# Feed-forward up projections of a decoder trunk as seven Strassen block products, on one Trainium2 core

## The reference

```python
D_MODEL = 1024; SEQ = 512; DEPTH = 2; DEC_BATCH = 8; N_A = 1
D_FF = 2816
def swiglu_ffn(x, w_in, w_out):
    gate, up = jnp.split(x @ w_in, 2, axis=-1)      # w_in 1024 x 5632
    return (jax.nn.silu(gate) * up) @ w_out         # w_out 2816 x 1024
def run(x, ...):
    for l in range(DEPTH):
        if l == N_A:
            kv = rms_norm(x, kv_norm) @ w_kv        # k (with rope) and v
        x = x + 0.5 * swiglu_ffn(rms_norm(x, norm_ffn[l, 0]), ffn_w_in[l, 0], ffn_w_out[l, 0])
        h = rms_norm(x, norm_mix[l])
        mix = conv_module(h, ...) if l < N_A else diff_attention(rope(h @ w_q), k, v) @ w_o
        x = x + mix
        x = x + 0.5 * swiglu_ffn(rms_norm(x, norm_ffn[l, 1]), ffn_w_in[l, 1], ffn_w_out[l, 1])
    return rms_norm(x, norm_final), ...
```

## Time and profile before

| | us |
|---|---|
| median of 3 runs | 2078.97 (2078.32 to 2080.6) |
| span of the profiled execution | 2076.1 |
| PE busy | 2031.0 (98%) |
| DVE busy | 916.6 (44%) |
| ACT busy | 677.6 (33%) |
| POOL busy | 500.2 (24%) |

### The profile page before, as it was taken

One profiled execution on the slowest core, in us unless ns is written; L12 is line 12 of the kernel. 1 busy time (PEld: TensorE's weight loads), 2 busy tenths in 40 slices (PEclk: granted clock), 3 DMA queues, 4 the chain that ended last, 5 costly groups with the idle time before them and its releaser, 6 DMA issues.

```text
span 2076.1 us, 39794 instructions
## 1 busy us (share of the span) xinstructions
PE 2031.0 (98%) x16292; PEld 1959.6 (94%) x16292; DVE 916.6 (44%) x1087; ACT 677.6 (33%) x1083; POOL 500.2 (24%) x343
## 2 busy tenths in 40 slices
PE   8999999999799999999999999999988999999998
PEld 7999999988599999999999999999965799999997
DVE  5444333499853333333543333333578543333323
ACT  4222222455542222222233222222256432222211
POOL 1333310133123333210312333300321223333210
PEclk9999999999999999999999999999999999999999
DMA  6333333288333333332553333322676133333331
GB/s 198 92 91 91 102 98 94 75 163 169 75 92 92 91 91 91 108 98 68 155 144 101 91 91 91 114 86 84 184 233 225 41 92 91 91 91 97 100 98 42
DMA packets 358735, 224.19 MB, mean 108 GB/s; under 512 B 8035, under 2 KB 342244, under 8 KB 358508
## 3 DMA queue, kind: packets, MB, share of 16 engines
q1 hardware_dynamic: 340836, 193.89, 31.5%
q0 software_dynamic: 8496, 18.93, 4.7%
q10 hardware_dynamic: 9320, 10.20, 1.7%
HBM read 198.52 MB, written 7.53 MB: 99 GB/s over the span
## 4 chain that ended last, share of the span: by engine, by line
PE 87%; DVE 7%; issue 2%; DMA 2%; ACT 1%; POOL 0%; DVEq 0%; ACTq 0%; SPq 0%; POOLq 0%
PE ps_all L567 84%; DVE conv_b L1390 1%; DVE conv L1390 1%; DVE kprod L1586 1%; DVE s_dec L1592 1%; PE ps_all L742 1%; PE ps_all L692 1%; DMA made<-made 1%; PE ps_all L660 1%; DVE w_lo L1208 1%; DVE nmx L1522 0%; DMA made<-sq 0%; DMA x<-xT 0%; DVE x L1336 0%; PE ps_all L624 0%
## 5 line engine op out<-in xcount | busy, mean ns | idle before, releaser
L873 ACT ACTIVATE w_hi<-raw 128x1024 fp32r<-128x1024 f32 (+1 forms) x295 | 333.5, 1130 | 1223.3 <-PE ps_all L567 1208.2
L567 PE MATMUL ps_all<-xg_hi,w_hi 128*128 128x260 f32 x3456 | 700.4, 284 | 10.0 <-DVE xg_lo L1218 9.0
L567 PE MATMUL ps_all<-xg_hi,w_lo 128*128 128x260 f32 x3456 | 697.3, 283 | 0.0
L567 PE MATMUL ps_all<-xg_lo,w_hi 128*128 128x260 f32 x3456 | 696.3, 283 | 0.0
L567 PEld LDWEIGHTS ps_all<-xg_hi,w_hi 128*128 128x128 f32 x3456 | 534.6, 189 | 12.2 <-issue 10.1
L567 PEld LDWEIGHTS ps_all<-xg_hi,w_lo 128*128 128x128 f32 x3456 | 533.7, 189 | 0.0
L567 PEld LDWEIGHTS ps_all<-xg_lo,w_hi 128*128 128x128 f32 x3456 | 532.5, 189 | 0.0
L1208 DVE TENSOR_TENSOR w_lo<-raw,w_hi 128x1024 fp32r<-128x1024 f32 (+1 forms) x295 | 397.1, 1346 | 259.1 <-ACT w_hi L873 259.1
L567 PE MATMUL ps_all<-h_hi,w_hi 128*128 128x260 f32 x1664 | 343.7, 284 | 7.0 <-DVE h_lo L1457 6.7
L567 PE MATMUL ps_all<-h_hi,w_lo 128*128 128x260 f32 x1664 | 341.3, 283 | 0.0
L567 PE MATMUL ps_all<-h_lo,w_hi 128*128 128x260 f32 x1664 | 340.7, 282 | 0.0
(11 more groups left out here) (204 smaller groups left out, 1106.7 us busy)
## 6 DMA issues: line engine op xcount, KB each, us to landing
raw<-w_in SPq DMA_DIRECT2D x175, 512.0 KB, 3.7
raw<-w_out SPq DMA_DIRECT2D x64, 704.0 KB, 4.2
made<-made POOLq DMA_DIRECT2D x41, 256.0 KB, 5.7
raw<-c_in SPq DMA_DIRECT2D x16, 512.0 KB, 3.8
raw<-w_kv SPq DMA_DIRECT2D x16, 512.0 KB, 3.9
page<-cache_k SPq DMA_DIRECT2D x16, 512.0 KB, 4.4
page<-cache_v SPq DMA_DIRECT2D x11, 512.0 KB, 5.5
t_out<-t_gate ACTq DMA_DIRECT2D x64, 65.0 KB, 2.7
```

The lines of the kernel that those rows point to most:

```text
L567: mm = nc.tensor.matmul(unit[slot][:, s, :], w[:, c % 2, k * P:(k + 1) * P], m[:, s * HALF:(s + 1) * HALF], start=kk == 0 and i == 0, stop ...
L873: nc.scalar.activation(w_hi[:, c % 2, 0:w], raw[:, c, 0:w], ACT.Copy).then_inc(hi_made, 1)
```

## The change

The up projections are computed by the Strassen-Winograd scheme. The product of `w_in` (split into rows (input features) and columns (gate, up)) and of x (split into feature halves and token halves) is a 2x2 block product. It is made of seven block products, whose operands are sums of blocks, and seven additions of results. The 1/rms factor of the gate is applied at the output, as before; that of the up side is no longer multiplied in by POOL but applied to the result of down, in which the hidden tiles are linear.

**Groups and items.** A group makes two gate and two up tiles. It has seven items (`product`), one per block product, each of 4 feature pairs x 3 products x 2 output tiles = 24 matmuls of 260 columns: 168 per group, where the same outputs took 192. Each item takes one w_hi, w_lo buffer of a ring of three. A feed-forward part has 11 groups, in three parts of 8, 8 and 6 hidden tiles (4, 4 and 3 groups), each followed by its own down phase of 8 chunks with 8, 8 or 6 tiles: up, down, up, down, up, down. Each down phase adds into x.

**Token sums.** For each of four pairs of x tiles, ACT copies both tiles into `stage` (`copy_x`), DVE makes four sums there (N1, T3, N2, T4; `combine_x`, 128x260 each), ACT rounds all seven operands (`combos_hi`, 1820 elements per partition) and DVE makes the rests (`combos_lo`). There is one `stage`: the next pair begins when the rests are done. The last pair goes in five segments.

**Weight sums.** Five loads of 512 KB per group (block W21 twice), then four accumulating DMAs of 512 KB by POOL: S3 = W21 + W11 and S1 = W21 + W22 when the loads are in, S2 = W11 + S1 when item 0 is split, S4 = W12 + S2 when item 1 is split and S2 is done. There are 10 slots, two sets of five; slots 0 to 3 of the first set are also the ring of the plain chunks. A slot is filled again once the last item that reads it has been split (`FREED_BY`). The groups of a feed-forward part take the second set and the first in turn, the second first (in the first part of the third feed-forward part the first set first), so that the last group of a part of 4 has the first set, and that of a part of 3 the second; there it is the other way round. After item n ACT and DVE split item n+2 (`step`), which needs the ring's buffer of item n-1.

**Results.** DVE takes PSUM in seven additions per group (`add`, 128x2x260), then gate times rstd, the product with `up_sum` and the rest h_lo, each for two tiles at once; ACT copies the first product, makes SiLU and rounds. POOL does no arithmetic in these phases. In down, DVE takes each chunk times rstd and adds it in a second instruction. All hardware loops are written out.

```diff
+PARTS = (8, 8, 6)
+PART_AT = (0, 8, 16)
+RING = 3
+PAIRS = KD // 2
...
+N1, N2, T3, T4, B21, B22, B11, B12 = range(8)
+STEPS_OF = (B11, B21, T3, N2, N1, T4, B22)
+SEGMENTS = ((B11, B12), (B21, B11), (T3, T4), (N1, T3), (T4, B21))
+SEGMENT_OF = (0, 1, 2, 3, 3, 4, 1)
+TAKEN_BY = (None, 1, 3, 2, 5, 6, 7)
+IN_A_SET = PAIRS - 1 + len(SEGMENTS)
...
+        W11, S1, W22, S3, W12 = range(5)
+        BLOCK_OF = (W11, W12, S3, W11, S1, W22, W12)
+        FREED_BY = {S3: 2, S1: 4, W22: 5, W11: 6, W12: 6}
...
+                for blk in (W11, S3, S1, W22, W12) if first_in else (S3, S1, W22, W11, W12):
+                    s = blk + 5 * in_second(ph, g)
...
+                    need[s] = ph.chunk0 + ITEMS * g + FREED_BY[blk] + 1
+            for c in range(ph.chunks):
+                s = c % 4
+                filled[s] += 16
+                landed[ph.chunk0 + c] = (s, filled[s])
+                of_phase.append((s, need[s], ph.weights(c)))
+                need[s] = ph.chunk0 + c + 1
...
+        def bank_of(g, i):
+            return (0, 2, 4, 6, 2, 0, 4)[i] if g % 2 == 0 else (6, 2, 4, 0, 2, 6, 4)[i]
...
+            def product(ph, g, i, q, pairs=range(PAIRS)):
+                n, room = ph.chunk0 + ITEMS * g + i, rooms[ph.f]
+                bank, ring = bank_of(g, i) + q, n % RING
+                if pairs[0] == 0 and q == 0:
+                    pe.wait_ge(weights_ready, n + 1)
+                    if i < 2 and not g:
+                        if ph.unit0:
+                            pe.wait_ge(drained, ph.unit0 - 1 + i)
+                    elif i < 4 and g:
+                        pe.wait_ge(taken, sums_of(ph, g - 1, (5, 4, 6, 5)[i]) if i else sums_of(ph, g - 1, 3))
+                    elif i == 5:
+                        pe.wait_ge(p1_copied, ph.group0 + g + 1)
+                    elif i in (4, 6):
+                        pe.wait_ge(taken, sums_of(ph, g, 1 if i == 4 else 2))
+                for j in pairs:
+                    if g == 0 and ph.part == 0:
+                        pe.wait_ge(xg_ready, READY_BEFORE[ph.set] + j + 1 + (SEGMENT_OF[i] if j == PAIRS - 1 else 0))
+                    hi, lo = room.x_hi[:, j, STEPS_OF[i], :], room.x_lo[:, j, STEPS_OF[i], :]
+                    for k, (w, m) in enumerate(((w_hi, hi), (w_hi, lo), (w_lo, hi))):
+                        mm = nc.tensor.matmul(ps_all[:, bank, 0:HALF], w[:, ring, j * GW + q * P:j * GW + (q + 1) * P], m,
+                                              start=j == 0 and k == 0, stop=j == PAIRS - 1 and k == 2)
+                if pairs[-1] == PAIRS - 1 and q:
+                    mm.then_inc(chunk_used, 1)
...
+                                for q in range(2):
+                                    product(ph, g, i, q, late)
+                            if fresh(ph):
+                                variance(sums, (rstd_made, made) if made else None, ps_stat_up)
+                        else:
+                            for i in range(2):
+                                for q in range(2):
+                                    product(ph, g, i, q)
+                        for i in range(2, ITEMS):
+                            if i == 3 and g == 0 and ph.part == 0:
+                                pe.wait_ge(rstd_made, made + fresh(ph))
+                                if ph.f == 2:
+                                    pe.wait_ge(v_copied, KD)
+                            for q in range(2):
+                                product(ph, g, i, q)
...
+                        act.wait_ge(raw_full[s], full)
+                    else:
+                        act.wait_ge({2: s3_added, 3: s2_added, 4: s1_added, 6: s4_added}[item.i][second], adds_of(ph, g))
+                if n >= RING:
+                    act.wait_ge(chunk_used, n - RING + 1)
+                nc.scalar.activation(w_hi[:, n % RING, 0:width], src, ACT.Copy).then_inc(hi_made, 1)
...
+                for g in range(ph.groups):
+                    for i in range(ITEMS):
+                        step(ph.chunk0 + ITEMS * g + i)
+                        if g and i == 1:
+                            silu(g - 1)
+                        elif g and i == 2:
+                            hidden_hi(g - 1)
+                        elif not g and i == 1 and fresh(ph):
+                            root(ps_stat_up)
+                        if i == 1:
+                            copy_p1(g)
+                silu(ph.groups - 1)
+                hidden_hi(ph.groups - 1)
 
...
+                def add(g, k, out, a, i, last=None):
+                    if last is not None:
+                        dve.wait_ge(chunk_used, ph.chunk0 + ITEMS * g + last + 1)
+                    b = bank_of(g, i)
+                    nc.vector.tensor_tensor(out, a, ps_all[:, b:b + 2, 0:HALF], ALU.add).then_inc(taken, 1)
+                def gate_first(g):
+                    dve.wait_ge(p1_copied, ph.group0 + g + 1)
+                    add(g, 1, t_gate[:, :, first], t_gate[:, :, second], 1, 1)
...
+                for g in range(ph.groups):
+                    n = ph.chunk0 + ITEMS * g
+                    step(n)
+                    if g:
+                        gate_second(g - 1)
+                        gate(g - 1)
+                    step(n + 1)
+                    if g:
+                        hidden(g - 1)
+                    elif fresh(ph):
+                        rms(ps_stat_up)
+                    step(n + 2)
+                    if g:
+                        hidden_lo(g - 1)
+                    step(n + 3)
...
+                        dve.wait_ge(v_turned, KD)
+                        dve.wait_ge(vs_copied, KD)
+                    gate_first(g)
+                    step(n + 4)
+                    thirds(g)
+                    step(n + 5)
+                    up_second(g)
+                    step(n + 6)
+                    up_first(g)
+                g = ph.groups - 1
+                gate_second(g)
+                gate(g)
+                hidden(g)
+                hidden_lo(g)
...
+                link(nc.vector.tensor_tensor(t_gate[:, 1, cols], unit[1][:, half, :], rstd[:, cols], ALU.mult))
...
+                    if ph.kind == "down":
+                        scaled(tm, m % 2).then_inc(drained, 1)
+                        dve.wait_ge(drained, ph.unit0 + m + 1)
+                        nc.vector.scalar_tensor_tensor(xm, tm, 0.5, xm, ALU.mult, ALU.add).then_inc(x_made, 1)
...
+                        if s in (2, 6):
+                            pair_lo(s, m)
...
+                        sums = SUMS_BEFORE[key] + KD
+                        dve.wait_ge(squared, SQUARES_BEFORE[key] + KD)
+                        dve.wait_ge(summed, sums - 1)
+                        nc.vector.tensor_tensor(acc[:, :], acc[:, :], sq[:, m % 2, :], ALU.add).then_inc(summed, 1)
+                        step(n)
...
-                dve.wait_ge(vs_copied, KD)
+                for m in range(KD):
+                    step(ph.chunk0 + m)
+                    pair_sums(4, m)
+                    pair_lo(4, m)
...
+            def add_more(ph, g):
+                n, second = ph.chunk0 + ITEMS * g, in_second(ph, g)
+                pool.wait_ge(weights_ready, n + 1)
+                pool.wait_ge(s3_added[second], adds_of(ph, g))
+                pool.wait_ge(s1_added[second], adds_of(ph, g))
+                add(ph, g, W11, S1, s2_added)
+                pool.wait_ge(weights_ready, n + 2)
+                pool.wait_ge(s2_added[second], adds_of(ph, g))
+                add(ph, g, W12, W11, s4_added)
 
...
                     for m in range(KD):
+                        if m == KD - 1:
+                            add_pairs(ph.next, 0)
...
+                    add_pairs(ph.next, 0)
+                    add_more(ph.next, 0)
```

More of the change, by code:

```diff
@@ L1435, in conv_in @@
                 gate(0, 0)
[L1436 removed]
+                for g in range(KD // 2):
+                    body(g)
                 a = conv[:, KD - 1, 0:SEQ]
```

910 lines of the change are left out of this document (506 added, 404 removed).

## The result

| | before | changed |
|---|---|---|
| median | 2079.78 us | 2140.53 us (2139.42 to 2141.18) |
| ratio, 95% interval | | 1.0295 (1.028 to 1.031) |
| span of the profiled execution | 2076.1 us | 2137.6 us |

The account below looks back on a forecast made before the run. The prediction took PE, 98% busy, to bound the kernel: -126.8 us for removed matmuls, against new waits at the start, handovers, groups and end and a slower clock, summed to +20, or 2099 us; range 2052 to 2142.

Follow-up runs that it names:

- the version with seven edits: Changed kernel with down's slots reordered, last two tiles later, freeing addition earlier, item 1's split first, two stages, variance later, W12 early: 2036.5 us, 0.9803 to kernel before.

## What to carry to other kernels

Cutting the matmuls of a kernel that PE bounds at 98% brings their worth only if each new dependency has PE work in front of it: count, for each place where PE changes to operands that were just made, the chain of instructions behind the last product against the matmuls that can run meanwhile, and reorder PE's own work first (two chunks' ready tiles, then both chunks' last ones, gave back 56 of 61 us). Here a wait of 3 us or more between full stretches, and some shorter ones, cost some 2 us again through the clock. When one wait is taken away, look at what it hid: at the start, at the variance and behind v most came back at the next late operand.

## What the runs showed of the hardware

In all the traces the granted clock fell behind every wait of 3.0 us or more, except among the first waits at the start, where PE had done little yet. Behind shorter ones it fell in some places and traces only: behind 1.77 us in the trace of the version with seven edits (the wait that ended at 1450.42), behind 2.43 us in some. The 2.8 us wait of the third feed-forward part's first handover was followed by a fall in the changed kernel, and by none in the traces with the splits first, without adds and with the variance later, which have it unchanged. At the handovers the clock then stayed low for some 3 to 5 us of work. Matmuls that nobody reads, put into the waits, held it at 1.00 and were worth 20 us. A 512 KB adding DMA between places in SBUF took 4.4 us at the least and 6.6 at the median from issue to landing (12.4 at most), close to the 5.9 of 256 KB ones before.
